# A two-block transformer on one core: Hyena spectra loaded earlier, the position network in halves, a head's memory softmax in one batch

## The chip, the core and the metric

The kernel runs on one core of a Trainium2 chip. A time is the device time of one execution in microseconds; runs of one kernel are compared by their median. TensorE (PE in the rows) does the matmuls; VectorE (DVE), ScalarE (ACT) and GpSimd (POOL) work on tiles beside it; SyncE (SP) issues all DMAs from one queue, in order. Each engine runs its own program in order and meets the others only at semaphores.

## The reference, cut to what matters

All is float32, 512 tokens by 1024 features. The first block: a hybrid mixer, a memory attention, a squared-ReLU MLP. The second: latent attention with a convolutional feed-forward network, then a Hyena mixer with another. The change touches five places:

```python
u = a * jax.nn.sigmoid(g)                      # short-convolution branch of the hybrid mixer
u = causal_depthwise_conv(u, conv_w, conv_b)   # 31 taps
log_f = jax.nn.log_sigmoid(f_logit + b_forget)
...
q = (h @ w_mq).reshape(B, S, MEM_HEADS, MEM_HEAD_DIM)       # memory attention: 4 heads, 256 slots
logits = jnp.einsum("bqhd,bmhd->bhqm", q, k) * (MEM_HEAD_DIM ** -0.5)
p = jax.nn.softmax(logits, axis=-1)
out = jnp.einsum("bhqm,bmhd->bqhd", p, v)
...
h = jnp.sin(freq * (z @ fw1 + fb1))            # Hyena position network, 64 wide, 512 positions
h = jnp.sin(freq * (h @ fw2 + fb2))
h = jnp.sin(freq * (h @ fw3 + fb3)) @ fw_out
...
u = dwconv_centred(x @ w_in, w_short)          # Hyena input and its width-3 convolution
v, g1, g2 = jnp.split(u, 3, axis=-1)
for o, gate in enumerate((g1, g2)):
    k_f = jnp.fft.rfft(two_sided_kernel(...), n=n)
    y = jnp.fft.irfft(jnp.fft.rfft(z, n=n) * k_f, n=n)[:, :length]
    z = gate * (y + d_bias[o] * z)
```

## The kernel before, in words

Features lie on the 128 partitions and tokens along the free axis, mostly in tiles of 128x512. Every product of float32 matrices is three matmuls of rounded halves (`mm3`, L127): each operand is split in a high part, which ACT copies, and a low part, which another engine gets by subtraction. All weights come in chunks of up to 1 MB (`CHUNKS`, numbered in the order of use) through two buffers: SP loads a chunk to `W32`, ACT makes `WH`, POOL makes `WL`; for chunks in `SHARED`, DVE makes the second half of `WL` (its `weights`). The load of chunk n waits until the low part of chunk n-2 is made, and ACT's copy waits until PE has used chunk n-2. Nothing is scheduled: the order on each engine is the order in which the functions `tensor_program`, `scalar_program`, `vector_program`, `pool_program` and `sync_program` write it, and a wait stops all that stands behind it on its engine.

The places, in order of time. **Position network** (0 to 21 us): three layers, each one matmul of 64x512 on PE (plain float32), three DVE instructions that reduce the angle (`layer`) and a sine on ACT (`sine`); the third sine is split to `H3H` and `H3L`, and `make_h` multiplies it with the output weights. POOL makes these weights (`wp`, `wp_low`) meanwhile. From it the filters and their spectra are computed (to 112 us), and the spectra are stored in memory as `kd`. **Forget gate** (112 to 152 us): PE makes the eight logits `f`, DVE scales them to `FZ`, PE turns them (`turn_f`), and DVE and ACT compute the log-sigmoid, whose cumulative sum is the matmul `cum`. This lies beside the first chunks of `win_ag` (numbers 2 to 5). In `gemm`, the argument `after` is called when a tile is complete, `between` after each step over k of the first chunk; `turn_f` is passed as `after`. **Memory attention** (451 to 512 us): `mem_q` makes the queries of a head, `mem_s` its logits in four blocks of 128x256, `mem_soft` and `mem_exp` the softmax, `mem_t` turns the probabilities, `mem_pv` multiplies with the values. There is one probability tile `PM`. DVE takes block after block: maximum, scale, wait for ACT's exponential, reciprocal, multiply; ACT can do the next block only after DVE has found its maximum. **Hyena** (1560 to 1860 us): twelve chunks `hy_in` with the width-3 convolution on DVE (`hyu`), then for each of two orders o: the transform of z (`dft_z`, 16 groups `zf` of six matmuls), the product with the spectrum on DVE (four instructions for each of eight pieces (m, c)) with sums to `YF` on POOL, and the inverse transform (`dft_i`). The product reads `KB[m % 2]` (1 MB each, in place of `X`, which is parked in memory as `xd` before) and, for m = 0, `KX`; both are loaded from `kd`. Piece (m = 2) waits for a load that may be issued when m = 0 is done. SP's program names chunks by number: it loads up to number 118, then `KX`, 119 and the four `KB` of order 0, then 120, `KX`, 121 and the four `KB` of order 1. The numbers stand for other chunks than the text around them suggests: `dft_z` and `dft_i` are 116 to 119 and `hy_o` is 120 to 123.

Of the kernel before, what the change touches and what calls it, by code (L numbers as in the profile page):

```python
# [63 lines left out]
CH = {}  # L64
# [5 lines left out]
SHARED = {n for n in range(1, len(CHUNKS)) if CHUNKS[n - 1][2] < 1000 or CHUNKS[n][:2] == ("hy_o", 1)}  # L70

# [175 lines left out]
def build(nc, t):  # L247
# [9 lines left out]
    with es:  # L257
# [82 lines left out]
        PM = sb("PM", A + 88, [128, 4, 256])  # L340
# [39 lines left out]
        KX = sb("KX", A + 112, [128, 1024])  # L380
# [43 lines left out]
        def tensor_program(pe):  # L424
# [180 lines left out]
            gemm("ag", CH["win_ag"][0:2], 8, 2, feat, lambda k: ("hn", 0, k), turn_f)  # L605
# [144 lines left out]
            def mem_s(h):  # L750
                for i in range(4):
                    ps = open_bank("ms_", h, i)
                    pe.wait_ge(*at("qm", h))
                    pe.wait_ge(*at("km", h))
                    pe.mm3(ps[:, 0:256], QMH[:, h, blk(i)], QML[:, h, blk(i)], KMH[:, h, :], KML[:, h, :],
                           True, True).then_inc(*up(acc, ("ms_", h, i)))

            def mem_t(h):
                for j in range(2):
                    ps = open_bank("mt", h, j)  # L760
                    for i in range(4):
                        pe.wait_ge(*at("mp", h, i))
                        ins = pe.turn(ps[:, blk(i)], PM[:, i, blk(j)], IDT[:])
# [258 lines left out]
        def scalar_program(act):  # L1022
# [1732 lines left out]
```

## Time and profile before

| | us |
|---|---|
| median of 3 runs (2318.22 to 2323.59) | 2319.98 |
| the profiled execution | 2320.62 |
| its span, first to last instruction | 2318.8 |
| PE busy | 2122.0 |
| DVE busy | 1324.6 |
| POOL busy | 946.0 |
| ACT busy | 836.1 |

Busy is the time in which an engine works on an instruction; a wait stands in square brackets behind the row of the instruction that waited, with the engine and tile that ended it. The mean granted TensorE clock is 0.939 of full speed (2.4 GHz).

### The profile page before, as it was taken

To read this page: it belongs to the slowest core of one execution; us is meant where nothing else is said; L and a number is where in the kernel's file an instruction comes from. 1 tells how busy PE (TensorE), PEld (TensorE's weight loads), DVE (VectorE), ACT (ScalarE), POOL (GpSimd) and SP (SyncE) were. 2 spreads that over 40 slices of the span, in tenths; PEclk is the share of its full clock that TensorE was granted. 3 is DMA by queue.
4 is the path that set the end of the run, shared out by engine and by line. 5 is a ranking of instruction groups with operands and counts; after the bars stand their busy time and mean duration, and the time that the engine had idled before them with its cause. 6 is when DMAs were issued, how large, how long until landed. Compare 5 with 4: busy or idle time off the path is not lost.

```text
span 2318.8 us, 23115 instructions
## 1 busy us (share of the span) xinstructions
PE 2122.0 (92%) x9475; PEld 1725.2 (74%) x9475; DVE 1324.6 (57%) x1631; ACT 836.1 (36%) x1175; POOL 946.0 (41%) x388
## 2 busy tenths in 40 slices
PE   7989988778999998899989999999987789999997
PEld 4667766667888886677778887877866677888786
DVE  6756762544324543456267776536656837777744
ACT  4623454444122223467243333223321224333322
POOL 4243124616444436211434434434655544334432
PEclk9989778888999998999999999989988898999998
DMA  5322111201222222111212222223231221322230
GB/s 179 142 85 75 46 37 55 91 26 66 104 96 91 93 107 71 39 32 53 73 55 91 91 100 100 91 73 122 95 138 68 105 73 55 101 99 91 94 106 37
DMA packets 34558, 194.02 MB, mean 84 GB/s; under 512 B 3903, under 2 KB 4495, under 8 KB 14932
## 3 DMA queue, kind: packets, MB, share of 16 engines
q1 hardware_dynamic: 34452, 192.54, 23.8%
q8 instruction: 75, 1.23, 0.2%
q14 instruction: 31, 0.25, 0.0%
HBM read 178.82 MB, written 13.64 MB: 83 GB/s over the span
## 4 chain that ended last, share of the span: by engine, by line
PE 59%; DVE 23%; ACT 11%; POOL 4%; issue 2%; DMA 1%; SPq 0%; DVEq 0%; POOLq 0%; ACTq 0%
PE ps L127 53%; DVE TMP L156 9%; DVE TMP L162 6%; PE ps L126 5%; ACT WH L143 4%; ACT TMP L144 1%; POOL WL L150 1%; DVE TMP L150 1%; DVE X L150 1%; ACT PAD L143 1%; POOL X L150 1%; DVE VG L150 1%; PE ps L135 1%; POOL YF L150 1%; DMA KB<-kd 1%
## 5 line engine op out<-in xcount | busy, mean ns | idle before, releaser
L150 POOL TENSOR_TENSOR WL<-W,WH 128x2048 fp32r<-128x2048 f32 (+3 forms) x175 | 710.1, 4062 | 1063.5 <-ACT WH L143 1063.5
L127 PE MATMUL ps<-HH,WL 128*128 128x512 f32 x1456 | 587.3, 403 | 64.3 <-ACT WH L143 18.2
L127 PE MATMUL ps<-HL,WH 128*128 128x512 f32 x1456 | 578.9, 398 | 0.0
L127 PE MATMUL ps<-HH,WH 128*128 128x512 f32 x1456 | 577.8, 397 | 0.0
L143 ACT ACTIVATE WH<-W 128x2048 fp32r<-128x2048 f32 (+2 forms) x157 | 291.8, 1859 | 322.0 <-PE ps L127 322.0
L127 PEld LDWEIGHTS ps<-HH,WL 128*128 128x128 f32 x1456 | 281.2, 193 | 137.3 <-issue 50.8
L127 PEld LDWEIGHTS ps<-HH,WH 128*128 128x128 f32 x1456 | 280.5, 193 | 60.8
L127 PEld LDWEIGHTS ps<-HL,WH 128*128 128x128 f32 x1456 | 281.3, 193 | 56.8 <-issue 0.2
L150 DVE TENSOR_TENSOR MRL<-MID,MRH 128x512 fp32r<-128x512 f32 x76 | 177.4, 2366 | 162.4 <-ACT MRH L143 162.4
L156 DVE TENSOR_SCALAR TMP<-PAD,PAR 128x512 f32<-128x512 f32 x88 | 208.9, 2374 | 70.6 <-ACT PAD L143 70.6
L127 PE MATMUL ps<-MRH,WL 128*128 128x512 f32 x608 | 238.4, 392 | 4.5 <-DVE TMP L162 2.2
L127 PE MATMUL ps<-MRH,WH 128*128 128x512 f32 x608 | 236.6, 389 | 0.0
L127 PE MATMUL ps<-MRL,WH 128*128 128x512 f32 x608 | 236.6, 389 | 0.0
L127 PEld LDWEIGHTS ps<-MRH,WL 128*128 128x128 f32 x608 | 114.1, 188 | 30.1 <-ACT PAD L143 3.0
L162 DVE SCALAR_TENSOR_TENSOR TMP<-PAD,PAR,TMP 128x512 f32<-128x512 f32 x176 | 132.3, 752 | 6.2
L127 PEld LDWEIGHTS ps<-MRH,WH 128*128 128x128 f32 x608 | 114.1, 188 | 24.1
L127 PEld LDWEIGHTS ps<-MRL,WH 128*128 128x128 f32 x608 | 114.1, 188 | 23.7 <-issue 0.5
L143 ACT ACTIVATE PAD<-ps 128x512 f32<-128x512 f32 x88 | 51.9, 590 | 193.4 <-PE ps L127 193.3
L150 POOL TENSOR_TENSOR TMP<-TMP,TMP 128x512 f32<-128x512 f32 x54 | 71.0, 1315 | 81.4 <-ACT TMP L144 79.3
L168 DVE RECIPROCAL SM<-SM 128x4 f32<-128x4 f32 (+2 forms) x46 | 7.9, 171 | 161.5 <-ACT SM L144 140.6
L162 DVE SCALAR_TENSOR_TENSOR X<-X,ps 128x512 f32<-128x512 f32 x32 | 22.0, 687 | 128.6 <-PE ps L127 128.4
L144 ACT ACTIVATE TMP<-TMP 128x512 f32<-128x512 f32 (+1 forms) x51 | 32.2, 632 | 157.5 <-DVE TMP L162 142.9
(337 smaller groups left out, 3159.4 us busy)
## 6 DMA issues: line engine op xcount, KB each, us to landing
W<-in_up SPq DMA_DIRECT2D x44, 1024.0 KB, 4.8
W<-in_down SPq DMA_DIRECT2D x22, 1024.0 KB, 4.8
W<-in_w_up SPq DMA_DIRECT2D x16, 1024.0 KB, 4.8
W<-in_w_down SPq DMA_DIRECT2D x16, 1024.0 KB, 4.8
W<-in_hy_in SPq DMA_DIRECT2D x12, 1024.0 KB, 4.9
kd<-STG SPq DMA_DIRECT2D x36, 256.0 KB, 2.0
KB<-kd SPq DMA_DIRECT2D x8, 1024.0 KB, 6.2
W<-in_win_ag SPq DMA_DIRECT2D x4, 1024.0 KB, 5.2
```

The costliest lines, as they stand in the source:

```text
L126: return self.eng.matmul(out, lhs, rhs, start=start, stop=stop, skip_group_check=True)
L127: return self.eng.matmul(out, lhs, rhs, start=start, stop=stop)
L135: return QUIET if self.eng is None else self.eng.transpose(out, src, ident)
L143: return self.eng.activation(out, src, fn, scale=scale)
L144: return self.eng.activation(out, src, fn, scale=scale, bias=bias)
L150: return QUIET if self.eng is None else self.eng.tensor_tensor(out, a, b, op)
L156: return self.eng.tensor_scalar(out, a, s1, None, o1)
L162: return self.eng.scalar_tensor_tensor(out=out, in0=a, scalar=s, in1=b, op0=o1, op1=o2)
L168: return QUIET if self.eng is None else self.eng.reciprocal(out, src)
```

## The change

Five edits.

1. SP loads the Hyena spectra earlier: the first `KB` and the `KX` of order 0 behind the sixth `hy_in` load, the second `KB` behind the seventh, `KX` and the first two `KB` of order 1 ahead of `dft_i` of order 1. Chunks are now named by `CH[...]`, not by number. `KX` has a tile of its own for each order, and `xd` is stored one chunk earlier.
2. The two `dft_i` chunks are in `SHARED`: POOL makes half of their `WL` and DVE the other half, ahead of its products.
3. The position network works on two halves of 256 columns, and the angle is kept in the matmul's bank.
4. `turn_f` is passed as `between`, and ACT copies chunk 3 ahead of the log-sigmoid.
5. Memory attention: two blocks of logits share a bank, one maximum instruction covers two blocks, the scale, the reciprocal and the exponentials of a head each go as a batch, the multiplication by the reciprocal is ACT's (`mem_norm`), `PM` is doubled, and the heads overlap more.

```diff
+SHARED |= set(CH["dft_i"])
...
-        PM = sb("PM", A + 88, [128, 4, 256])
+        PM = [sb(f"PM{i}", A + (72, 88)[i], [128, 4, 256]) for i in range(2)]
...
-        KX = sb("KX", A + 112, [128, 1024])
+        KX = [sb(f"KX{o}", (36, A + 112)[o], [128, 1024]) for o in range(2)]
...
             for l in range(3):
+                for c in range(2):
+                    p = slice(256 * c, 256 * c + 256)
...
+                        pe.wait_ge(*at("sin", l - 1, c))
...
+                    pe.mm(ps[0:64, 0:256], lhs, rhs, True, True).then_inc(*up(acc, ("mlp", l, c)))
...
-            gemm("ag", CH["win_ag"][0:2], 8, 2, feat, lambda k: ("hn", 0, k), turn_f)
+            gemm("ag", CH["win_ag"][0:2], 8, 2, feat, lambda k: ("hn", 0, k), between=turn_f)
...
             mem_s(0)
             mem_q(2)
+            mem_s(1)
+            mem_t(0)
+            mem_q(3)
             for h in range(4):
-                mem_t(h)
+                if h < 2:
+                    mem_s(h + 2)
+                mem_pv(h)
                 if h < 3:
-                    mem_s(h + 1)
-                if h == 0:
-                    mem_q(3)
-                mem_pv(h)
+                    mem_t(h + 1)
...
             sine(0)
+            sine(1)
             wp_high(0, 0, 0)
-            sine(1)
+            sine(2)
+            for c in range(2):
+                p = slice(256 * c, 256 * c + 256)
+                act.wait_ge(*at("sin", 2, c))
+                high(H3H[:, p], TMP[0][0:64, p], ("fh3", c))
             wp_high(0, 0, 1)
-            sine(2)
-            act.wait_ge(*at("sin", 2))
-            high(H3H[:], TMP[0][0:64, :], ("fh3",))
...
             scale_out(0)
+            weights(3)
...
-            weights(3)
             gate(0)
...
+            def mem_norm(h):
+                for i in range(4):
+                    s, p = 32 * (h % 2) + 168 + i, PM[h % 2][:, i, :]
+                    act.wait_ge(*at("rcp", "ms_", h))
+                    act.act(p, p, ACT.Identity, SM[:, s:s + 1]).then_inc(*out(("mp", h, i)))
...
+                for c in range(2):
+                    p = slice(256 * c, 256 * c + 256)
+                    arg, kq = bank("mlp", l, c)[0:64, 0:256], TMP[4][0:64, p]
...
+                s = 32 * (h % 2) + 160
+                for b in range(2):
+                    dve.wait_ge(*at("ms_", h, b))
+                    dve.rmax(SM[:, s + 2 * b:s + 2 * b + 2],
+                             bank("ms_", h, b)[:].rearrange("p (a c) -> p a c", a=2)).then_inc(*out())
+                dve.wait_ge(*now(dve_tile))
+                dve.tt(SM[:, s:s + 4], SM[:, s:s + 4], SM[:, 24:28], ALU.mult).then_inc(*out(("max", "ms_", h)))
+                dve.wait_ge(*at("exp", "ms_", h, 3))
+                dve.recip(SM[:, s + 8:s + 12], SM[:, s + 4:s + 8]).then_inc(*out(("rcp", "ms_", h)))
...
             for o in range(2):
+                weights(CH["dft_i"][o])
                 for m in range(4):
...
+            load_kb(0, 0)
+            load_kx(0)
+            weights(first + 6)
+            load_kb(0, 1)
+            weights(*range(first + 7, CH["dft_i"][0] + 1))
+            load_kb(0, 2)
+            load_kb(0, 3)
+            weights(CH["dft_z"][1])
+            load_kx(1)
+            load_kb(1, 0)
+            load_kb(1, 1)
+            weights(CH["dft_i"][1])
+            load_kb(1, 2)
+            load_kb(1, 3)
+            weights(*CH["hy_o"][0:2])
```

The order of instructions at three places. First ACT, from the end of the spectra to the first sigmoid; `WH_52` and `WH_53` are the high parts of chunks 2 and 3, the three `SM` rows of 128x32 the log-sigmoid. Before:

```order
L143 ACTIVATE WH_52<-W_0_50 128x2048
L144 ACTIVATE SM<-ps,PAR 128x4
L143 ACTIVATE TMP_67<-ps 128x512
L144 ACTIVATE SM<-SM 128x32
L144 ACT_TABLE_LOAD
L144 ACTIVATE SM<-SM 128x32
L144 ACT_TABLE_LOAD
L144 ACTIVATE SM<-SM,PAR 128x32
L143 ACTIVATE WH_53<-W_1_51 128x2048
L144 ACT_TABLE_LOAD
L144 ACTIVATE TMP_63<-TMP_63 128x512
```

And with the change:

```order
L144 ACTIVATE WH_52<-W_0_50 128x2048
L145 ACTIVATE SM<-ps,PAR 128x4
L144 ACTIVATE TMP_67<-ps 128x512
L144 ACTIVATE WH_53<-W_1_51 128x2048
L145 ACTIVATE SM<-SM 128x32
L145 ACT_TABLE_LOAD
L145 ACTIVATE SM<-SM 128x32
L145 ACT_TABLE_LOAD
L145 ACTIVATE SM<-SM,PAR 128x32
L145 ACT_TABLE_LOAD
L145 ACTIVATE TMP_63<-TMP_63 128x512
```

The copy of chunk 3 has moved past the three log-sigmoid instructions and their two table loads. On PE the transposes of `FZ`, on whose result the log-sigmoid waits, stood at the end of the 48 matmuls of chunk 2:

```order
L127 MATMUL ps<-HH,WH_52 128x512
L135 MATMUL ps<-IDT,FZ 128x8 x4
L127 MATMUL ps<-HH,WL_54 128x512
L127 MATMUL ps<-HL,WH_52 128x512
L127 MATMUL ps<-HH,WH_52 128x512
L135 MATMUL ps<-IDT,EB 128x16
L127 MATMUL ps<-HH,WL_55 128x512
```

With the change they stand behind its first six matmuls, and those of `EB` six further on:

```order
L128 MATMUL ps<-HH,WH_52 128x512
L136 MATMUL ps<-IDT,FZ 128x8 x4
L128 MATMUL ps<-HH,WL_54 128x512
L128 MATMUL ps<-HL,WH_52 128x512
L128 MATMUL ps<-HH,WH_52 128x512
L128 MATMUL ps<-HH,WL_54 128x512
L128 MATMUL ps<-HL,WH_52 128x512
L128 MATMUL ps<-HH,WH_52 128x512
L136 MATMUL ps<-IDT,EB 128x16
```

Last SP, around the Hyena spectra; `W_0_50` and `W_1_51` are the two `W32` buffers, `KB_185` and `KB_186` the two `KB`. Before, from the last `hy_in` load to the first two `KB` of order 1:

```order
L180 DMA W_1_51<-in_hy_in 128x2048
L180 DMA W_0_50<-in_dft_z 128x2048
L180 DMA W_1_51<-in_dft_i 128x2048
L180 DMA W_0_50<-in_dft_z 128x2048
L180 DMA KX<-kd 128x1024
L180 DMA W_1_51<-in_dft_i 128x2048
L180 DMA KB_185<-kd 128x2x1024
L180 DMA KB_186<-kd 128x2x1024
...
L180 DMA W_0_50<-in_hy_o 128x2048
L180 DMA KX<-kd 128x1024
L180 DMA W_1_51<-in_hy_o 128x2048
L180 DMA KB_185<-kd 128x2x1024
```

With the change, where `KB_187` and `KB_188` are the same two tiles, from the sixth `hy_in` load on:

```order
L181 DMA W_1_51<-in_hy_in 128x2048
L181 DMA KB_187<-kd 128x2x1024
L181 DMA KX_179<-kd 128x1024
L181 DMA W_0_50<-in_hy_in 128x2048
L181 DMA KB_188<-kd 128x2x1024
...
L181 DMA W_1_51<-in_dft_i 128x2048
L181 DMA KB_187<-kd 128x2x1024
L181 DMA KB_188<-kd 128x2x1024
L181 DMA W_0_50<-in_dft_z 128x2048
L181 DMA KX_180<-kd 128x1024
L181 DMA KB_187<-kd 128x2x1024
L181 DMA KB_188<-kd 128x2x1024
L181 DMA W_1_51<-in_dft_i 128x2048
```

The first two `KB` of order 0 stood behind the load of 119, whose buffer is free when POOL has split chunk 117; those of order 1 behind that of 121, whose buffer is free when POOL has split chunk 119. Now neither does.

## Rows read from the trace of the kernel before

**Rows 1.** The page, part 1: busy time, share of the span, instructions.

```profile
PE 2122.0 (92%) x9475; PEld 1725.2 (74%) x9475; DVE 1324.6 (57%) x1631; ACT 836.1 (36%) x1175; POOL 946.0 (41%) x388
```

**Rows 2.** A stretch: busy PE, PEld, DVE, ACT, POOL; granted clock, DMA share, GB/s.

```profile
470.00:515.00 45.00, 32.59 (x147) 26.01 (x146) 24.80 (x71) 21.75 (x46) 5.05 (x2) 0.85 0.07 24
```

**Rows 3.** Timeline of the start: start, us, engine, instruction, [idle before, releaser].

```profile
3.54 1.94 PE L127 MATMUL ps<-TMP,SM 33*64 33x512 f32 x2 [3.54 <-DMA TMP<-in_zfeat]
...
6.42 0.42 DVE L156 TENSOR_SCALAR TMP<-TMP 64x512 f32<-64x512 f32 x1
...
8.28 1.96 PE L127 MATMUL ps<-TMP,SM 64*64 64x512 f32 x2 [2.81 <-ACT TMP L144]
9.87 2.48 POOL L150 TENSOR_TENSOR STG<-FW 64x512 f32<-64x512 f32 x2 [9.43 <-DMA FW<-in_fw_out]
...
11.19 1.45 DVE L156 TENSOR_SCALAR TMP<-TMP 64x512 f32<-64x512 f32 x1
...
15.01 1.96 PE L127 MATMUL ps<-TMP,SM 64*64 64x512 f32 x2 [4.78 <-ACT TMP L144]
...
21.41 0.79 PE L127 MATMUL ps<-WPH,H3L 64*128 64x512 f32 x1 [4.43 <-DVE H3L L150]
```

**Rows 4.** Groups by form, ACT: busy us, mean ns of one.

```profile
L143 ACT ACTIVATE HM<-TMP 128x256 fp32r<-128x256 f32 x8 | 3.3, 417 | 7.3 <-DVE TMP L162 7.3
```

**Rows 5.** Groups by form, DVE.

```profile
L150 DVE TENSOR_TENSOR KML<-ps,KMH 128x256 fp32r<-128x256 f32 x4 | 1.5, 418 | 0.7 <-ACT KMH L143 0.7
```

**Rows 6.** Timeline of chunk 2's low part.

```profile
111.85 1.22 DVE L150 TENSOR_TENSOR WL<-W,WH 128x1024 fp32r<-128x1024 f32 x1 [3.48 <-ACT WH L143]
111.89 3.38 POOL L150 TENSOR_TENSOR WL<-W,WH 128x1024 fp32r<-128x1024 f32 x1 [2.37 <-ACT WH L143]
```

**Rows 7.** Timeline of the forget gate, chunks 2 and 3.

```profile
127.31 0.41 PE L135 MATMUL ps<-IDT,FZ 8*128 8x8 f32 x4
...
131.49 1.89 ACT L143 ACTIVATE WH<-W 128x2048 fp32r<-128x2048 f32 x1
...
138.06 0.76 PE L127 MATMUL ps<-HH,WL 128*128 128x512 f32 x1 [9.29 <-ACT WH L143]
...
138.62 0.63 PE L127 MATMUL ps<-HL,WH 128*128 128x512 f32 x1
...
142.73 0.40 PE L127 MATMUL ps<-HH,WH 128*128 128x512 f32 x1
```

**Rows 8.** Groups by form, memory attention (466 to 513 us): exponential, its sum, maximum.

```profile
L141 ACT ACTIVATE PM<-ps,SM 128x256 f32<-128x256 f32 x16 | 9.0, 565 | 19.4 <-DVE SM L157 19.4
...
L141 ACT ACTIVATION_READ_ACCUMULATOR PM<-ps,SM 128x1 f32 x16 | 3.1, 191 | 0.0
...
L171 DVE TENSOR_REDUCE SM<-ps 128x1 f32<-128x256 f32 x16 | 6.7, 416 | 0.0
```

**Rows 9.** Timeline of memory attention, last two heads.

```profile
493.70 0.33 PE L135 MATMUL ps<-IDT,PM 128*128 128x128 f32 x1 [1.52 <-DVE PM L156]
...
510.34 0.63 PE L127 MATMUL ps<-OMH,WL 128*128 128x512 f32 x1
```

**Rows 10.** Timeline of Hyena, order 0.

```profile
1705.77 4.80 POOL L150 TENSOR_TENSOR WL<-W,WH 128x2048 fp32r<-128x2048 f32 x1 [6.08 <-ACT WH L143]
...
1711.28 0.90 SPq L180 DMA_DIRECT2D KB<-kd  x2
...
1718.39 1.88 DVE L150 TENSOR_TENSOR TMP<-ps,KB 128x512 f32<-128x512 f32 x3 [12.27 <-DMA KB<-kd]
1719.76 2.51 POOL L150 TENSOR_TENSOR YF<-TMP,TMP 128x512 f32<-128x512 f32 x2 [9.19 <-DVE TMP L150]
```

**Rows 11.** Timeline of Hyena, order 1.

```profile
1785.14 4.60 POOL L150 TENSOR_TENSOR WL<-W,WH 128x2048 fp32r<-128x2048 f32 x1 [3.75 <-ACT WH L143]
...
1797.77 1.89 DVE L150 TENSOR_TENSOR TMP<-ps,KB 128x512 f32<-128x512 f32 x3 [13.78 <-DMA KB<-kd]
```

**Rows 12.** Tile KB: time from issue to landing.

```profile
DMA to landing us min/median/max: 4.8/6.2/9.3
```

More of the change, by code:

```diff
@@ L1331, in mem_exp, with mem_turned @@
             def mem_exp(h):
+                slot = 32 * (h % 2) + 160
                 for i in range(4):
-                    need = [("mt", h - 1, 1)] if h else []
-                    expo(("ms_", h, i), PM[:, i, :], 256, SM[:, 20 + i:21 + i], 32 * (h % 2) + 160, *need)
-            mq_high(0)
-            mq_high(1)
-            root(("st", 1), 0, "eps6")
-            mem_exp(0)
-            mq_high(2)
-            for h in range(4):
+                    if h >= 2:
+                        act.wait_ge(*at("mt", h - 2, 1))
+                    act.wait_ge(*at("max", "ms_", h))
+                    act.act(PM[h % 2][:, i, :], bank("ms_", h, i // 2)[:, 256 * (i % 2):256 * (i % 2) + 256], ACT.Exp,
+                            SM[:, 20 + i:21 + i], SM[:, slot + i:slot + i + 1], SM[:, slot + 4 + i:slot + 5 + i]).then_inc(
+                        *out(("exp", "ms_", h, i), *[("free", "ms_", h, i // 2)] * (i % 2)))
+            def mem_norm(h):
[3 more added lines that the diff above has]
+                    act.act(p, p, ACT.Identity, SM[:, s:s + 1]).then_inc(*out(("mp", h, i)))
+            def mem_turned(h):
                 for j in range(2):
@@ L1346, in scalar_program, with mem_out @@
                     high(PMH[:, j, :], bank("mt", h, j)[:], ("pm", h, j))
-                if h < 3:
-                    mem_exp(h + 1)
-                if h == 0:
-                    mq_high(3)
+            def mem_out(h):
                 act.wait_ge(*at("mo", h))
                 high(OMH[:, h, :], bank("mo", h)[:], ("om", h))
+            mq_high(0)
+            mq_high(1)
+            root(("st", 1), 0, "eps6")
+            mem_exp(0)
+            mem_norm(0)
+            mq_high(2)
+            mem_exp(1)
+            mem_turned(0)
+            mem_norm(1)
+            mq_high(3)
+            for h in range(4):
+                if h < 2:
+                    mem_exp(h + 2)
+                mem_out(h)
+                if h < 3:
+                    mem_turned(h + 1)
+                if h < 2:
+                    mem_norm(h + 2)
             roots_next()
@@ L1719, in vector_program @@
                 layer(l)
-            low(H3L[:], TMP[0][0:64, :], H3H[:], ("fh3",))
+            for c in range(2):
+                p = slice(256 * c, 256 * c + 256)
+                low(H3L[:, p], TMP[0][0:64, p], H3H[:, p], ("fh3", c))
             for n in range(17):
@@ L2542, in sync_program, with load_kx, load_kb @@
             load("pos", POSI[:], t["pos"])
-            weights(*range(60, 108))
+            def load_kx(o):
+                for k in (8, 9, 26, 27)[2 * o:2 * o + 2]:
+                    sp.wait_ge(*at("kd", k))
+                for i in (22, 23):
+                    if o:
+                        sp.wait_ge(*at("hyu", i))
+                sp.dma(KX[o][:], KD[o, 8]).then_inc(*up(kx_land, ("kx", o), by=16))
+            def load_kb(o, m):
+                if m >= 2:
+                    sp.wait_ge(*at("kbu", o, m - 2))
+                elif o:
+                    sp.wait_ge(*at("kbu", 0, m + 2))
+                else:
+                    sp.wait_ge(*at("xs"))
+                for k in range(36):
+                    sp.wait_ge(*at("kd", k))
+                sp.dma(KB[m % 2][:].rearrange("p (a c) -> p a c", a=2),
+                       KD[o, 2 * m:2 * m + 2].rearrange("a p c -> p a c")).then_inc(
+                    *up(kb_land[m % 2], ("kb", o, m), by=16))
+            first = CH["hy_in"][0]
+            weights(*range(60, first + 3))
             for k in range(8):
@@ L2572, in sync_program @@
             load("xl", X[:], XD)
[L2573 removed]
+            weights(*range(CH["hy_o"][2], len(CHUNKS)))
             for k in range(8):
```

111 lines of the change are left out of this document (45 added, 66 removed).

## The prediction

> **What bounds the kernel now.** First the page's busy times: PE works for 2122.0 of 2318.8 us and no other engine for more than 1325 [rows 1]. No matmul of size is removed, so only the 197 us in which PE stands idle can be won, and an edit on DVE, ACT or POOL counts where PE waits for it. Then the timelines of the five places, read for the idle time in front of PE's instructions. At the start PE's three layers begin at 3.54, 8.28 and 15.01 and the first filter matmul at 21.41; each waits for ACT's sine or DVE's `H3L` [rows 3]. In the forget gate PE stops for 9.29 us at 138.06, for `WH` of chunk 3, which ACT began only at 131.49 [rows 7]. In memory attention PE works 32.59 of 45 us [rows 2] and waits 1.52 us for one block of `PM` after the other [rows 9]. In Hyena's two orders DVE stands 12.27 and 13.78 us for `KB` alone [rows 10, 11], and POOL's sums and the inverse transform behind it.
>
> **Hyena (gain 21.2).** In order 0 the low part of chunk 117 runs 1705.77 to 1710.57, the first `KB` is issued at 1711.28, and the products start at 1718.39 [rows 10]. With the load some 60 us ahead, DVE has all it needs when it falls idle, at 1718.39 − 12.27 = 1706.12. The change gives it half of `WL` first: 1.22 for 1024 columns [rows 6], so it is ready at about 1707.4. POOL, which makes the first sum 1.37 us behind the first product (1719.76), takes 3.38 for its half in place of 4.80 [rows 6, 10] and is free at 1705.77 + 3.38 = 1709.15. So the first sum comes at 1709.15 and not 1719.76: 10.6. In order 1 the low part starts at 1785.14, is done at 1788.5, and the first sum stood at 1797.77 + 1.37 = 1799.14 [rows 11]: again 10.6. Without the split (4.80 and 4.60) each would be 9.2 to 9.4. What is late next is `KB` for m = 2: it may be issued when m = 0 is done and is needed after m = 1, and a piece (m, c) takes DVE some 2.7 us, its three products of 1.88 [rows 10] and the one with `KX`; that cover is some 6.6 us with the queue's delay, for a landing of 4.8 to 9.3 [rows 12]. It was so before too, so I take no change; if transfers now collide, up to 9.3 − 6.6 = 2.7 each time. The four loads moved ahead, and the store of `X`, lie among loads of `hy_in`, where POOL waits 6.08 us for work [rows 10]: a `KB` of 9.3 us at the worst could push one chunk by 3.2 us, which stands under rivals. Sum 21.2, with bounds 17 (one late landing of 2.7 and 1.5 lost elsewhere) and 22.
>
> **Forget gate (gain 11.3).** `turn_f` after six matmuls instead of 48: DVE's `FZ` is ready by about 116, PE gets there near 118, and each transpose group is 0.41 [rows 7], as before. ACT's copy of chunk 3 no longer stands behind a chain that begins with those transposes at 127.31; it follows the scaling at 115.4, runs 1.89, and is done near 117.3. POOL's full `WL` of 4.80 (that of another chunk of the same size [rows 10]) then ends near 122, and PE is through with chunk 2 at 138.06 − 9.29 = 128.77. So the whole 9.29 goes. After the stall PE ran ten matmuls slow: they last 0.63 where the later ones last 0.40, and start 0.43 apart in place of 0.23, from 138.06 to the one at 142.73 [rows 7]: 2.0. Sum 11.3. Next late: chunk 4's copy waits until PE has used chunk 2, at 128.8, not for the log-sigmoid; two chunks take it and POOL 1.89 + 4.80 = 6.7, to 135.5, and PE needs it at about 141. The log-sigmoid itself now runs beside chunk 3, with 20 us until `cum`. At the least 9 (POOL's copy slips and the slow stretch stays), at the most 12.
>
> **Position network (gain 6.1).** A layer now has two halves. To the first half's sine: PE about 1.1 (half of the 1.94 for 512 columns, and a start) [rows 3]; three DVE instructions of 256 columns, priced by one that reads 256 columns of a bank, 0.42 [rows 5], with gaps 1.46; a sine of 256 columns at 0.42 [rows 4], with its wait 0.5. Together 3.1, and DVE is occupied 2.92 for both halves, just inside it. Three layers from 3.54: 12.9; the second half follows 1.5 later, at 14.4; the splits `H3H` and `H3L` of a half take 0.42 each, so both halves are ready at 15.3, against 21.41 [rows 3]. Before, a layer took 8.28 − 3.54 = 4.74 alone, and 6.73 once POOL worked beside it: the same DVE instruction went from 0.42 at 6.42 to 1.45 at 11.19, with POOL's 2.48 from 9.87 [rows 3]. I take that this slowing doesn't come back, since the half instructions read at most one operand outside the bank; if it does, 2 us of the gain go (4). The spectra, ACT's first copies and the rest start as much earlier, and no load of the first 16 us is waited for. Bounds 4 and 7.
>
> That the slowing goes agrees with the Trainium skill, "SBUF — State Buffer", section on the two separate sides: VectorE and GpSimd take their common port pair as an exclusive lock, held by a VectorE operation in a two-port mode or with two SBUF inputs, and one with a single SBUF input outside those modes doesn't contend. The rows show the slow pair; that a bank operand frees it, none shows. Against the change speaks its page "VectorE: DVE Perf Modes", section on why PSUM operands drop a tier: a PSUM operand takes the fast mode from a float32 instruction. The trace agrees: 0.42 buys 512 columns in SBUF [rows 3] but 256 from a bank [rows 5]. An estimate by that rule is some 0.15 us lost on each layer's second instruction; it is within the 0.42 above.
>
> **Memory attention (gain 6.0).** Before, a head costs four times a chain of maximum 0.416, scale, exponential 0.565 and its sum 0.191, reciprocal, multiply [rows 8]; PE sees it as 0.33 + 1.52 = 1.85 per block [rows 9], 7.4 a head. Now a head is two maxima over 512 columns (0.7 each, taken as less than two of 0.416), one scale 0.2, four exponentials with sums at about 0.62 = 2.5, one reciprocal 0.2, four multiplications on ACT at 0.42 [rows 4] = 1.6: 5.9 in a row. Each waits on shared ACT and DVE with three more copies per head (`mem_turned`, `mem_out`). Placed by the written order from 466.5 on, with matmuls unchanged: head 0 is turned at 474.0, head 1 at 483, head 2 at 491.4, head 3 at 497.7; `PML` of head 3 is ready at 502.3, and the first output matmul starts at 504.1, against 510.34 [rows 9]. Heads 2 and 3 leave PE idle some 4 and 2 us before their turns, so part of it runs at the lower clock, as before (mean 0.85 [rows 2]). Bounds 3 (an exponential costs its full 0.76, and multiplications 0.5: 0.9 a head on three heads) and 8 (clock stays up).
>
> **The sum.** 21.2 + 11.3 + 6.1 + 6.0 = 44.6. The profiled execution took 2320.62; 2320.62 − 44.6 = 2276.0. Its time is 0.64 above the median of the runs, so I say 2275.5. These stretches are apart in time and the rest of the program is written as before, so they add. Low bounds 17 + 9 + 4 + 3 = 33, high 22 + 12 + 7 + 8 = 49: 2271 to 2287 if all go one way, so 2272 to 2281 for this case.
>
> **Rivals.**
> - *The wait comes back in Hyena.* `KB` for m = 2 (or the order-1 load at its new place beside a weight load) lands after its need. For it: landings reach 9.3 us [rows 12]. Against it: the same loads stood there before. 2.7 us at each of two places, or one order's 10.6 lost to half: 2281 to 2286.
> - *Attention gives nothing.* The longer waits in one piece let the granted clock fall more often, and every copy on ACT queues behind a batch. For it: clock 0.85 already [rows 2], and ACT gets the multiplications. Against it: 7.4 against 5.9 a head. With start contention left: 2275.5 + 6 + 2 = 2283.5, range 2280 to 2286.
> - *More than counted.* Fewer stops keep PE at full speed beyond the ten matmuls, and the first half of the last layer lets PE begin before 15.3. 5 to 8 us more: 2268 to 2271.
> - *The change doesn't do what it says.* The loads are earlier but the products wait for something else that landed at the same time (`KX`, the store of `X`, a bank). Against it: both rows name `KB` [rows 10, 11]. 2297.
> - *Slower.* SP's queue is in order: `KB` and `KX` wait for the store of `X` and for the stored spectra, with the `hy_in` loads queued behind them, and ACT, POOL and PE wait for those. Two `KB` at 9.3 and one `KX` of half the size, with no slack, is 23 us on the path, and if the products of both orders still wait as before, the 21.2 isn't had: 2320 − 23.4 + 23 = 2320, and with 4 us of slower clock behind those stops 2324. It decides once a chunk comes 6.08 us late, where POOL's idle time ends [rows 10], and needs this at nearly every load.
>
> **How the numbers follow.** Main case 0.69, wait back in Hyena 0.11, attention 0.09, more 0.06, not what it says 0.02, the slower case 0.03. The time is the main case's, 2275.5. The range reaches from the favourable rival's 2268 to past the two nearest on the other side: 2266 to 2288 holds all but some 0.15. A measurement tells 0.2% (4.6 us) from no change: the slower case lies at 2320 to 2324, a third of it within that bound, so slower 0.02, same 0.01, faster 0.97.
>
> **What would show it.** Right: first filter matmul near 15.3; DVE's angle instructions near 0.42 also beside POOL; no `WH` wait of 9 us near 130; first output matmul of memory attention some 23.5 us earlier than 510.34 (near 487 with the two gains before it); no `<-DMA KB` ahead of a product with m = 0, and the first `YF` 3.4 us behind the start of POOL's half. Wrong: idle time of several microseconds on PE inside `hy_in`, new `<-DMA W` or `<-DMA KB` waits, or PE busy well above 2122 from a lower clock.

## The result and the profile after

| | us |
|---|---|
| before, median of 4 runs (2318.22 to 2323.59) | 2320.34 |
| changed, median of 4 runs (2281.91 to 2287.43) | 2285.58 |
| ratio, with its 95% interval | 0.9847 (0.983 to 0.9864) |
| the profiled execution of the changed kernel | 2287.43 |
| the same kernel run five times more later (2280.11 to 2286.90) | 2286.13 |

The forecast was 2275.5 with 2266 to 2288. Over all nine runs the changed kernel's median is 2286.13; that is the base for the experiments below. Against 2320 some 34 to 35 us are gained, where 44.6 were forecast. Part 1 of the page after, which answers to [rows 1]:

```profile
PE 2118.8 (93%) x9481; PEld 1725.2 (75%) x9481; DVE 1327.9 (58%) x1596; ACT 842.3 (37%) x1195; POOL 942.6 (41%) x388
```

PE's busy time is 3.2 us shorter; the other 30.0 of the 33.2 us by which the span is shorter (2318.8 to 2285.6) come out of its idle time. To see where, both executions are cut at the same matmuls: at numbers 0, 100, 200, 300, 400, 500, 1100 and 1200 of the matmuls of `HH` with `WL` (not shown: 300 to 400 took 68.0 in both, 500 to 600 and 600 to 1100 gave 1.1 and 1.3). The columns are the stretch, its length, busy time of PE, PEld, DVE, ACT and POOL, the granted clock of TensorE, the DMA share and GB/s. Before:

```profile
0.00:115.40 115.40, 96.39 (x359) 65.63 (x359) 82.13 (x123) 61.50 (x108) 40.50 (x31) 1.00 0.46 162
115.40:244.50 129.10, 117.55 (x472) 91.75 (x473) 76.19 (x125) 41.19 (x60) 43.60 (x14) 0.88 0.21 77
244.50:554.80 310.30, 255.32 (x1098) 205.99 (x1097) 158.12 (x286) 146.75 (x270) 124.38 (x62) 0.81 0.16 55
554.80:624.60 69.80, 69.80 (x317) 58.06 (x316) 30.45 (x37) 14.43 (x12) 29.02 (x7) 1.00 0.22 76
692.60:1107.40 414.80, 386.73 (x1787) 316.95 (x1786) 198.46 (x246) 184.50 (x288) 141.72 (x46) 0.98 0.20 68
...
1700.40:1993.00 292.60, 242.43 (x1200) 203.50 (x1198) 189.64 (x261) 80.36 (x97) 144.01 (x90) 0.90 0.25 90
1993.00:2318.80 325.80, 309.55 (x1395) 253.88 (x1394) 212.44 (x177) 102.20 (x117) 127.34 (x32) 0.98 0.26 88
```

And after:

```profile
0.00:111.50 111.50, 99.27 (x364) 67.92 (x364) 82.59 (x133) 62.23 (x113) 39.82 (x31) 1.00 0.48 167
111.50:229.80 118.30, 114.05 (x472) 89.40 (x473) 78.69 (x126) 41.52 (x60) 43.80 (x14) 0.93 0.23 83
229.80:530.70 300.90, 250.88 (x1098) 203.00 (x1097) 148.12 (x239) 151.11 (x285) 123.92 (x61) 0.82 0.16 56
530.70:604.20 73.50, 71.68 (x317) 59.17 (x316) 35.37 (x37) 14.76 (x12) 29.41 (x8) 0.98 0.22 74
672.20:1092.50 420.30, 393.01 (x1788) 321.70 (x1787) 199.07 (x246) 184.86 (x288) 141.72 (x46) 0.96 0.20 67
...
1683.10:1957.40 274.30, 236.67 (x1199) 200.62 (x1199) 194.34 (x263) 80.37 (x97) 140.95 (x90) 0.93 0.24 87
1957.40:2285.60 328.20, 311.86 (x1395) 256.29 (x1394) 212.57 (x177) 102.20 (x117) 127.40 (x32) 0.97 0.25 87
```

The four stretches that hold edits give 3.9 + 10.8 + 9.4 + 18.3 = 42.4. Three stretches in which nothing was edited take back 3.7 + 5.5 + 2.4 = 11.6, each with a lower clock than before. That second sum is what the forecast didn't have.

**Start.** PE's first filter matmul (21.41 before [rows 3]) and DVE's angle beside POOL, which works from 9.41:

```profile
9.88 0.42 DVE L157 TENSOR_SCALAR TMP<-ps 64x256 f32<-64x256 f32 x1
10.33 0.41 DVE L163 SCALAR_TENSOR_TENSOR TMP<-TMP,ps 64x256 f32<-64x256 f32 x1
...
15.17 0.79 PE L128 MATMUL ps<-WPH,H3L 64*128 64x512 f32 x1 [2.81 <-DVE H3L L151]
```

6.2 us earlier, and the DVE instructions aren't slowed. By 111.5 only 3.9 is left: behind the next stall (27.32; 33.54 before) fifteen matmuls took 0.63 us each, where five did before. The clock column shows 1.00 there all the same, so they are known as slow by their durations alone.

**Forget gate.** ACT's copy of chunk 3 begins at 111.48 and the transposes of `FZ` at 113.11, neither behind the other; the wait of 9.29 [rows 7] is gone. DVE's instruction at 115.39 took 0.17 before the change, with POOL idle; now it lies beside POOL's split of 113.47 to 118.06. And a new wait has come, at the matmul of the cumulative sum:

```profile
111.48 1.90 ACT L144 ACTIVATE WH<-W 128x2048 fp32r<-128x2048 f32 x1
...
113.11 0.41 PE L136 MATMUL ps<-IDT,FZ 8*128 8x8 f32 x4
...
115.39 2.70 DVE L157 TENSOR_SCALAR SM<-SM 128x32 f32<-128x32 f32 x1
...
136.47 2.31 PE L128 MATMUL ps<-TMP,SM 128*8 128x512 f32 x8 [1.94 <-DMA TMP<-in_consts]
```

**Memory attention.** The first output matmul stands at 488.27, against 510.34 [rows 9]: 22.1 earlier, of which 14.5 were there at the first logits (465.46 before, 450.97 after). So 7.6 is attention's own. One instruction sticks out, DVE's scale of head 1's maxima, of four columns:

```profile
459.75 4.60 POOL L151 TENSOR_TENSOR WL<-W,WH 128x2048 fp32r<-128x2048 f32 x1 [18.35 <-ACT WH L144]
...
462.10 2.26 DVE L151 TENSOR_TENSOR SM<-SM 128x4 f32<-128x4 f32 x1
...
488.27 0.40 PE L128 MATMUL ps<-OMH,WL 128*128 128x512 f32 x1
```

It ends at 464.36, POOL's at 459.75 + 4.60 = 464.35; in the other heads it takes 0.16. That one of the two engines waits like this until the other's instruction is over is what the expectations below call the port.

**Behind attention.** In the stretch of 73.5 us (69.8 before) stands the same thing on the path. DVE adds up eight squares, in seven sums; before, the last of them had begun when POOL began to split a chunk:

```profile
559.76 2.94 DVE L150 TENSOR_TENSOR Y<-Y 128x512 f32<-128x512 f32 x4
...
562.46 4.67 POOL L150 TENSOR_TENSOR WL<-W,WH 128x2048 fp32r<-128x2048 f32 x1 [6.33 <-ACT WH L143]
```

After, POOL began 0.01 us ahead of the last sum:

```profile
538.39 4.57 POOL L151 TENSOR_TENSOR WL<-W,WH 128x2048 fp32r<-128x2048 f32 x1 [5.87 <-ACT WH L144]
...
538.40 5.10 DVE L151 TENSOR_TENSOR Y<-Y 128x512 f32<-128x512 f32 x1
...
543.56 1.05 PE L127 MATMUL ps<-ONE,Y 128*128 128x1 f32 x8 [1.82 <-DVE Y L151]
```

**Hyena.** No product waits for `KB` any more. Order 0, which answers to [rows 10], and order 1, which answers to [rows 11]:

```profile
1688.54 2.59 POOL L151 TENSOR_TENSOR WL<-W,WH 128x1024 fp32r<-128x1024 f32 x1 [6.07 <-ACT WH L144]
1688.80 3.42 DVE L151 TENSOR_TENSOR WL<-W,WH 128x1024 fp32r<-128x1024 f32 x1
...
1692.14 1.87 DVE L151 TENSOR_TENSOR TMP<-ps,KB 128x512 f32<-128x512 f32 x3
...
1693.49 5.26 POOL L151 TENSOR_TENSOR YF<-TMP,TMP 128x512 f32<-128x512 f32 x4 [2.36 <-DVE TMP L151]
...
1758.12 1.23 DVE L151 TENSOR_TENSOR WL<-W,WH 128x1024 fp32r<-128x1024 f32 x1 [1.11 <-ACT WH L144]
1758.16 3.43 POOL L151 TENSOR_TENSOR WL<-W,WH 128x1024 fp32r<-128x1024 f32 x1 [3.75 <-ACT WH L144]
...
1761.78 1.29 DVE L151 TENSOR_TENSOR TMP<-ps,KB 128x512 f32<-128x512 f32 x2 [1.83 <-PE ps L128]
...
1762.55 5.26 POOL L151 TENSOR_TENSOR YF<-TMP,TMP 128x512 f32<-128x512 f32 x4 [0.95 <-DVE TMP L151]
```

From the start of the low part to the first sum it was 1719.76 − 1705.77 = 13.99, and in order 1 13.99 again (1797.77 + 1.36 − 1785.14). Now it is 4.95 and 4.39: 9.0 and 9.6 gained, where the forecast had 10.6 twice. The two halves aren't made side by side: whichever engine starts second takes longer by what the first still has to do (POOL's 2.59 and then DVE's 3.42; DVE's 1.23 and then POOL's 3.43). In order 1 PE's transform is late next, 1.83 us. `KB` lands no later than it did (4.8/6.2/9.3 before [rows 12]):

```profile
DMA to landing us min/median/max: 4.8/5.1/7.6
```

### The profile page after: what moved, and what is told of

It is laid out like the page before. It is cut to its first block, busy times and chain, and to the rows that moved or that the text cites. A ratio compares the mean times of both kernels' runs of the same rounds, so it can differ in the third digit from the quotient of the medians.

```text
span 2285.6 us, 23112 instructions
## 1 busy us (share of the span) xinstructions
PE 2118.8 (93%) x9481; PEld 1725.2 (75%) x9481; DVE 1327.9 (58%) x1596; ACT 842.3 (37%) x1195; POOL 942.6 (41%) x388
## 3 DMA queue, kind: packets, MB, share of 16 engines
q8 instruction: 75, 1.23, 0.2%
## 4 chain that ended last, share of the span: by engine, by line
PE 59%; DVE 23%; ACT 11%; POOL 4%; issue 2%; DMA 0%; SPq 0%; DVEq 0%; POOLq 0%; ACTq 0%
PE ps L128 54%; DVE TMP L157 9%; DVE TMP L163 6%; PE ps L127 5%; ACT WH L144 4%; DVE TMP L151 1%; ACT TMP L145 1%; POOL X L151 1%; POOL WL L151 1%; ACT PAD L144 1%; PE ps L136 1%; DVE X L151 1%; DVE VG L151 1%; POOL YF L151 1%; POOL TMP L151 1%
## 5 line engine op out<-in xcount | busy, mean ns | idle before, releaser
L169 DVE RECIPROCAL SM<-SM 128x4 f32<-128x4 f32 (+1 forms) x34 | 6.0, 176 | 155.2 <-ACT SM L145 136.4
L151 DVE TENSOR_TENSOR TMP<-ps,TMP 128x512 f32<-128x512 f32 x36 | 24.9, 690 | 113.8 <-PE ps L128 105.5
```

The lines of the kernel that those rows point to most:

```text
L151: return QUIET if self.eng is None else self.eng.tensor_tensor(out, a, b, op)
L169: return QUIET if self.eng is None else self.eng.reciprocal(out, src)
```

## The experiments

All twelve start from the changed kernel and are compared with its median of nine runs, 2286.1. Two theories went into the first four, which each put one part back. Theory 1: a part is worth what PE's start times show at its place. Theory 2: part of each gain is paid back later. Medians of four or five runs are compared with a base that itself spreads over 7.3 us, so a difference of a few microseconds is judged by the place in the profile and not by the time.

**1. Hyena put back.** The edit takes back the SP order, the second `KX` and the split of `dft_i`:

```diff
-SHARED |= set(CH["dft_i"])
-                weights(CH["dft_i"][o])
-            load_kb(0, 0)
-            load_kx(0)
 ...
+                weights(119 + 2 * o)
+                for m in range(4):
```

> The changed kernel with the Hyena part put back: SP loads the spectra in the old order, one KX, POOL makes the whole low part of the two dft_i chunks. Theory 1 (each part is worth what PE's local start times show in the profiled execution of the changed kernel): 19.6 us slower than the changed kernel, 2305 us, with a wait of DVE for KB of 12 to 14 us back in both orders. Theory 2 (part of each gain is paid back elsewhere by PE's lower clock in unchanged code): the loss is 12 to 16, 2298 to 2301. My prediction's own term would make it 21.2 slower, 2307.

Measured: 2303.0 (2297.65 to 2306.05), 16.9 slower; ratio to before 0.9923 (0.991 to 0.9936). The idle time of DVE ahead of products, us and times:

```profile
  DMA KB<-kd: 25.7, 2
```

The wait is KB's, as forecast, and the part is worth some 17, below the 18.3 of its stretch by no more than runs differ. That lies between the two theories (2305, and 2298 to 2301) and decides for neither. This is the largest term and nearly all of it arrives.

**2. Forget gate put back.**

```diff
-            gemm("ag", ..., between=turn_f)
+            gemm("ag", ..., turn_f)
             scale_out(0)
-            weights(3)
 ...
+            weights(3)
             gate(0)
```

> The changed kernel with turn_f again at the end of chunk 2 and ACT's copy of chunk 3 behind the log-sigmoid. Theory 1: 9.3 us of wait and 2 us of slow matmuls come back, the wait of 1.9 us for the triangle goes: 9.5 to 10 slower than the changed kernel, 2295. Theory 2: 5 to 8 slower, 2291 to 2293. The prediction's term: 11.3, 2297.

Measured: 2291.32 (2289.20 to 2293.47), 5.2 slower; ratio 0.9877 (0.9864 to 0.9891). The wait is back in full:

```profile
132.68 0.76 PE L128 MATMUL ps<-HH,WL 128*128 128x512 f32 x1 [9.30 <-ACT WH L144]
```

PE is 10.0 us later at 240 us (239.8 against 229.8) and still 10.3 at 682; the unedited stretch behind it takes 416.1 in place of 420.3, and at the end 3.9 are left in the profiled execution (2289.5 against 2285.6) and 5.2 in the medians. Theory 2 holds: half of what the place shows is gone by the end.

**3. Position network put back.**

```diff
-                for c in range(2):
-                    p = slice(256 * c, 256 * c + 256)
-                    ps = open_bank("mlp", l, c)
+                ps = open_bank("mlp", l)
```

> The changed kernel with the position network on all 512 columns, angle in TMP. Theory 1: the first filter matmul starts 6.2 us later, near 21.4, and the whole is 6 us slower, 2291.5. Theory 2: 12 matmuls that ran at the lower clock from 30.1 to 35.3 in the changed kernel run fast again, as before the change, which gives 2.4 back: 3.8 slower or less, 2288 to 2289.5.

Measured: 2287.39 (2286.97 to 2288.54), 1.3 slower; ratio 0.9862 (0.9847 to 0.9877). The first filter matmul and the unedited stretch that took 420.3 us in the changed kernel:

```profile
20.73 0.79 PE L128 MATMUL ps<-WPH,H3L 64*128 64x512 f32 x1 [4.44 <-DVE H3L L151]
```

```profile
677.50:1091.30 413.80, 385.70 (x1787) 315.91 (x1786) 198.45 (x246) 184.62 (x288) 141.72 (x46) 0.98 0.19 68
```

5.6 us later at the start, still 5.3 at 677, and 1.2 ahead of the changed kernel at 1091: the same code took 6.5 us less. My reason for theory 2 was wrong, though. The matmuls at 30 us didn't run fast again (fourteen slow, against fifteen); the difference came back a thousand microseconds later.

**4. Memory attention put back.**

```diff
-        PM = [sb(f"PM{i}", A + (72, 88)[i], [128, 4, 256]) for i in range(2)]
+        PM = sb("PM", A + 88, [128, 4, 256])
 ...
             for h in range(4):
-                if h < 2:
-                    mem_s(h + 2)
+                mem_t(h)
+                if h < 3:
+                    mem_s(h + 1)
+                if h == 0:
+                    mem_q(3)
                 mem_pv(h)
-                if h < 3:
-                    mem_t(h + 1)
 ...
```

> The changed kernel with memory attention as it was. Theory 1: the first output matmul comes 7.5 us later relative to the stage's start, and the whole is 7.5 slower, 2293. Theory 2: the new DVE wait behind attention (1.8 us at 543.6, where POOL works beside DVE's squares) and the slow matmuls near 545, 935 and 960 are consequences of attention's new timing, and go: 0 to 4 slower, 2286 to 2289. The prediction's term: 6.0, 2291.5.

Measured: 2288.89 (2287.22 to 2293.59), 2.8 slower; ratio 0.987 (0.9857 to 0.9883). The stage is 9.9 longer, but the one behind it takes 69.9 again, without the wait of 1.82. Theory 2 again: with the new attention the last sum of squares meets POOL's split. The profiled execution was the slowest of the four (2293.59), so the size of this part is known to a few microseconds only. The four parts cost 16.9 + 5.2 + 1.3 + 2.8 = 26.2 one at a time, and all together 34.

**5. The changed kernel again**, without an edit.

> The changed kernel itself, word for word, to say how far executions of one program differ and to give the four undone parts a firmer base. If the four losses (17.4, 5.7, 1.8 and 3.3, sum 28.2) fall short of the whole gain of 34.8 by an unlucky base, this median lies 1 to 3 us below 2285.6; if they fall short because the parts' gains don't add, it lies at 2285.6 within 1.

Measured: 2286.13 (2280.11 to 2286.90). The base wasn't unlucky, by the expectation's own test. That the parts don't add is less firm than the medians make it look: the nine runs seem to lie in two groups, two at 2280 to 2282 and seven at 2285 to 2287.5, and with means in place of medians the four parts cost 30 against 35 for all together, a difference that these few runs don't tell from none. What the traces do show are the places where a gain is lost again.

**6. The triangle first.**

```diff
-            weights(4, 5, 6)
+            weights(4, 5)
             sp.wait_ge(*at("rs", 0))
             load("tri", DG[:], t["consts"][:, 256:768])
+            weights(6)
```

> The changed kernel with the load of the triangle (the tile of the cumulative sum) moved ahead of the load of chunk 6. Theory: the wait of PE for it, 1.94 us at 136.5, is an effect of the forget gate's gain, since the load stands in SP's queue behind a load that waits for the split of chunk 4; it goes, and the whole is 1.9 us faster, about 2283.7. Rival: something else of the cumulative sum is late right behind it, and under 0.5 us is gained.

Measured: 2278.80 (2277.51 to 2279.19), 7.3 faster; ratio to before 0.9822 (0.9806 to 0.9837). The wait is gone, but 100 matmuls further on only 0.5 us of it is left (229.3 against 229.8), since more of them ran slow. The two unedited stretches, which took 73.5 and 420.3 in the changed kernel, gave 9.2, of which little was lost again behind them (the spans are 2277.0 and 2285.6):

```profile
530.60:600.40 69.80, 69.80 (x317) 58.08 (x316) 30.80 (x37) 14.76 (x12) 29.72 (x7) 1.00 0.23 77
668.40:1083.20 414.80, 386.74 (x1788) 316.84 (x1787) 198.48 (x246) 184.48 (x288) 141.72 (x46) 0.98 0.19 68
```

Here DVE's last sum began before POOL's split, and POOL waited for it (5.03 in place of 4.57). Neither theory in the expectation foresaw this: the edit moved what follows by a little (530.6 against 530.7 at the start of that stage), and the order of two engines turned.

**7. The scale of the maxima as four instructions.**

```diff
-                dve.tt(SM[:, s:s + 4], SM[:, s:s + 4], SM[:, 24:28], ALU.mult)...
+                for i in range(4):
+                    ins = dve.ts(SM[:, s + i:s + i + 1], SM[:, s + i:s + i + 1], SM[:, 24 + i:25 + i], None, ALU.mult)
```

> The changed kernel with the scaling of a head's maxima, one DVE instruction with two operands in SBUF (128x4), as four instructions with one each (128x1). Theory (the port): the 2.26 us that this instruction took at 462.1 while POOL split a chunk were a wait for POOL, and the four take 0.9 together there; attention gains about 1.4 there and loses 0.5 on each of the other heads, 0 to 1 us in sum. Rival (the instruction was slow for another reason, such as its operands being just written): the four take more than 2 us there as well.

Measured: 2284.03 (2283.21 to 2288.44), 2.1 less than the base, which four runs don't tell from no change; ratio 0.9849 (0.9832 to 0.9866). Head 1, in the midst of POOL's split:

```profile
465.21 0.58 DVE L157 TENSOR_SCALAR SM<-SM 128x1 f32<-128x1 f32 x4
```

0.58 for four in place of 2.26 for one: the theory holds and the rival falls. It doesn't follow that one operand in SBUF never waits. In the changed kernel a TENSOR_SCALAR of 128x32 from SBUF to SBUF took 2.70 beside POOL's split and 0.17 without (the row of 115.39), and run 10 shows another. From the first logits to the first output matmul it is 37.6 us, against 37.3: what head 1 gains, the other three heads' 0.4 each take back.

**8. POOL behind the last sum.**

```diff
             post(2, Y2)
+            pool.wait_ge(*at("hacc", 2, 7))
             weights(CH["w_down"][-1] + 1)
```

> The changed kernel with one wait more: behind memory attention POOL splits chunk 26 only when DVE has added the last of the eight squares, 0.7 us later. Theory (the port): the last add took 5.10 us at 538.4 because it began 0.01 us behind POOL's split of 4.57 us; it takes 0.68 again, PE's wait of 1.82 us at 543.6 and the slow matmuls behind it go, and the stage takes 69.9 us as before the change instead of 73.5: 3.6 faster, about 2282. Rival: the stage is longer for another reason (clock), and the kernel is the same or 0.7 slower.

Measured: 2282.57 (2280.15 to 2284.70), 3.6 faster; ratio 0.9839 (0.9821 to 0.9856). DVE's seven sums, POOL's split, and the stage:

```profile
534.07 5.11 DVE L151 TENSOR_TENSOR Y<-Y 128x512 f32<-128x512 f32 x7
...
539.27 4.60 POOL L151 TENSOR_TENSOR WL<-W,WH 128x2048 fp32r<-128x2048 f32 x1 [6.65 <-DVE Y L151]
```

```profile
530.70:600.60 69.90, 69.90 (x318) 58.09 (x316) 31.03 (x37) 14.75 (x12) 29.52 (x8) 1.00 0.22 77
```

A wait added to an engine with time to spare gives 3.6 us back to PE: shown at the place. The time agrees, but all four runs, two near 2280.3 and two near 2284.7, lie inside the base's own spread, and run 9 shows a larger difference from an edit worth 0.1; the time alone proves little. The unedited stretch behind 668 us took 419.8, nearly as in the changed kernel.

**9. `dft_i` not shared.**

```diff
-SHARED |= set(CH["dft_i"])
-                weights(CH["dft_i"][o])
```

> The changed kernel without the split of the two dft_i chunks: POOL makes the whole low part. Theory (the port): where POOL and DVE make a half each, they don't work at once, 2.59 and then 3.42 less the wait in order 0, so halves end 3.7 us after the start and not 3.38 or 1.22; POOL alone needs 4.6. The first sum of order 0 comes 0 to 0.3 us later, that of order 1 0.2 to 0.5 later, and the kernel is within 1 us of the changed one, 2285 to 2287. The prediction had the split worth 1.2 to 1.4 in each order: 2288.5.

Measured: 2280.81 (2279.43 to 2288.67), ratio 0.9835 (0.9812 to 0.9858). From the start of the low part to the first sum, in order 0:

```profile
1683.89 4.82 POOL L150 TENSOR_TENSOR WL<-W,WH 128x2048 fp32r<-128x2048 f32 x1 [6.07 <-ACT WH L143]
...
1688.67 2.53 POOL L150 TENSOR_TENSOR YF<-TMP,TMP 128x512 f32<-128x512 f32 x2
```

4.78, against 4.95 with the split; in order 1 4.66 against 4.39. By its places edit 2 is worth 0.1 us. The time lies 5 below the base, where 2285 to 2287 was expected, but 4.2 of it is again in the unedited stretch behind 672 us (416.1 us), so it is no verdict on the edit. Three of the four runs lie at 2279.4 to 2281.4 and one at 2288.7.

**10. The angle in SBUF.**

```diff
-                    arg, kq = bank("mlp", l, c)[0:64, 0:256], TMP[4][0:64, p]
+                    ps, kq = bank("mlp", l, c)[0:64, 0:256], TMP[4][0:64, p]
+                    arg = TMP[3 if l == 1 else 0][0:64, p]
 ...
```

> The changed kernel with the angle of the position network kept in TMP, halves of 256 columns as they are. Theory (the port): the second and third DVE instruction are faster until 9.4 us (the second near 0.25 in place of 0.42), and slow once POOL begins at 9.4, one of them taking over 1 us; the first filter matmul starts at 16 to 17.5 in place of 15.17. Rival (halves alone give the whole gain, and the bank is no help or a loss): it starts at 14.5 to 15.2.

Measured in one run: 2285.29. POOL works from 9.40 here:

```profile
9.54 1.26 DVE L157 TENSOR_SCALAR TMP<-TMP 64x256 f32<-64x256 f32 x1
10.84 1.36 DVE L163 SCALAR_TENSOR_TENSOR TMP<-TMP,TMP 64x256 f32<-64x256 f32 x1
...
17.47 0.79 PE L128 MATMUL ps<-WPH,H3L 64*128 64x512 f32 x1 [3.66 <-DVE H3L L151]
```

Without POOL the same two take 0.28 and 0.42; beside it 1.26 and 1.36, and the first filter matmul is 2.3 us later than with the angle in the bank. So of the 6.2 us at the start, the halves give 3.9 and the bank 2.3.

**11. The low parts of `dft_i` on DVE.**

```diff
+POOL_PART = {n: 16 for n in CH["dft_i"]}
-                h = cols // 2
+                h = POOL_PART.get(n, cols // 2)
```

> The changed kernel with the low parts of the two dft_i chunks made by DVE but for 16 columns. Theory (the port): DVE alone takes 2.3 to 2.4 us for 2032 columns, less than the 3.5 that DVE and POOL need for it together; the first sum of order 0 comes 0.9 us earlier, that of order 1 is unchanged, since PE's transform is late there (DVE waits for it until 1761.8): 0.5 to 1 us faster, 2285. Rival (the two engines do work side by side): it is 1 us slower in each order, 2288.

Measured: 2282.27 (2279.97 to 2284.07), ratio 0.9833 (0.9818 to 0.9847). Order 0:

```profile
1687.17 0.42 POOL L152 TENSOR_TENSOR WL<-W,WH 128x16 fp32r<-128x16 f32 x1 [6.07 <-ACT WH L145]
1687.43 2.29 DVE L152 TENSOR_TENSOR WL<-W,WH 128x2032 fp32r<-128x2032 f32 x1
...
1691.00 5.25 POOL L152 TENSOR_TENSOR YF<-TMP,TMP 128x512 f32<-128x512 f32 x4 [3.41 <-DVE TMP L152]
```

3.83 from the start to the first sum in place of 4.95, and 4.71 for 4.39 in order 1: 0.8 gained in sum, as expected, though order 1 was expected to stay. There POOL's 16 columns began behind DVE's 2032 and took 2.31. DVE alone takes 2.29 for what the two together took 3.7 for. The rest of the 3.9 by which the median is lower comes from elsewhere: the stage behind attention took 69.9, and other unedited stretches differ by 2 to 4 us both ways.

**12. All four mended.** The edits of runs 6, 8 and 11, and that of run 7 for head 1 alone.

> The changed kernel with four edits: the triangle loaded ahead of chunk 6, POOL's wait behind the last sum of squares, the scale of head 1 alone as four instructions, and the low parts of dft_i on DVE. Theory: no wait of 1.9 at 136 and none of 1.8 at 543; against the changed kernel (2286) it gains 1.9 + 3.6 + 0.9 + 0.5 = 6.9, 2279; if the stretch behind 690 us comes out with 13 slow matmuls as in the run with the triangle first, and not 33, up to 5 more, 2274. Rival: the run with the triangle first (2278.8) already had all that is to be had, and this one is at 2278 to 2279.

Measured: 2277.12 (2275.05 to 2279.52), 9.0 below the changed kernel; ratio to before 0.9811 (0.9797 to 0.9826). Against the run with the triangle first it is 1.7 less, which isn't told apart: that kernel had the good outcome at both far places already, and here the unedited stretch took 417.3. The median lies between the 2279 and the 2274 of the theory, and below those of both kernels.

## Why the prediction was right, and where its sum was off

The direction, the main mechanisms and all five places held, and the time is in the range, 10 us above the value. That it is in the range is in part luck. The prediction gave its main case 2272 to 2281, and 2285.6 is outside; it lies where two rivals stood, `KB` late again in Hyena (2281 to 2286) and attention without a gain (2280 to 2286), and neither of them happened. By its steps:

- **Position network, 6.1.** The place gave 6.2, and the first filter matmul stood at 15.17 (15.3 forecast). That POOL's slowing goes with the angle in the bank was taken without a row; run 10 shows it: 2.3 us (2 forecast). The Trainium skill, "SBUF — State Buffer", section on the two separate sides, says the same of two SBUF inputs and of the two-port modes, and the trace agrees: 1.26 and 1.36 beside POOL for 0.28 and 0.42 without it. Its other rule, in "VectorE: DVE Perf Modes", section on why PSUM operands drop a tier, holds too: the second instruction takes 0.28 from SBUF and 0.42 from the bank, 0.14 where 0.15 was estimated, a small price for being free of POOL. The rows that the prediction compared for this rule were of two kinds of instruction, a TENSOR_SCALAR [rows 3] and a TENSOR_TENSOR [rows 5]; the like pair is in run 10. Of the 6.2 us, 3.9 are left at 111.5.
- **Forget gate, 11.3.** 9.3 and the slow stretch went, as said. I looked for what is late next at chunk 4, and missed the triangle, whose load SP holds behind that of chunk 6: 1.9 of it came back as a wait. 10.8 by its stretch.
- **Memory attention, 6.0.** 7.6 at the place; the prediction's own placing gives 510.34 − 504.1 = 6.2. The step that failed stands behind it: "these stretches are apart in time and the rest of the program is written as before, so they add". The new timing put a sum of squares 0.01 us behind POOL's split, which costs 3.6 to 3.7 (runs 4 and 8). The stage took 73.5 to 73.6 in the profiles of the changed kernel and of runs 1, 2, 3, 5 and 9, and 69.8 to 69.9 in all others.
- **Hyena, 21.2.** 18.3 to 18.6. The failed price is the two halves of a low part, 1.22 on DVE and 3.38 on POOL, taken as done side by side. [Rows 6] showed these two numbers, and POOL's 3.38 already held DVE's 1.22: half of 4.6 is 2.3. With 2.3 for POOL alone I would have seen that the halves are made one after the other, and that the split is worth 0.1 and not 2.6. POOL's lock, and a transform that is late by 1.8 in order 1, are the difference.
- **The unedited stretches.** Besides attention's 3.7, the stretch from matmul 400 to 500 took 5.5 more and the last one 2.4 more, at a lower clock in both. In the profiled executions of the changed kernel and the twelve runs the first of them took 413.8 to 420.3 us with the same instructions; 14 to 34 of its matmuls took 0.60 to 0.66 us, where 0.40 is the usual time. PE's waits agree up to 271 us into this stretch; from there the next 22 us are, before and after:

```profile
964.30:986.30 22.00, 17.34 (x80) 12.86 (x79) 15.56 (x27) 12.85 (x22) 5.08 (x2) 1.00 0.17 51
943.90:965.90 22.00, 17.93 (x55) 12.46 (x54) 12.87 (x20) 9.98 (x15) 5.04 (x2) 0.69 0.16 51
```

After the change the granted clock fell from 2.4 to 1.2 GHz in parts of these 22 us (0.69 in the mean), and PE got through 55 matmuls in place of 80. The rival with a lower clock (0.09) was of this kind, but I put it into attention, where the clock didn't fall. Of the changed kernel's nine executions two were profiled, both at 420; that this stretch makes the two groups of its times is likely and not shown. What decides which outcome an execution gets stays open. That it depends on small shifts in what comes before is likely, since the edit of run 6, at 119 us, is followed by the shorter outcome and by times that lie within 1.7 us of each other, where the changed kernel's spread over 7.3; it takes more executions to show it.
- No chunk of `hy_in` was held up by the spectra's loads, and the slower rival found nothing: the stretch up to matmul 1100 in which these loads are issued (1594.5 to 1700.4 before the change, 1577.2 to 1683.1 after) took 105.9 in both.

## What to carry to other kernels

Local gains of a few microseconds, read from an engine's start times, aren't what the whole kernel gains: the places showed 42 us here and 34 arrived, while a wait of 1.9 us taken away in run 6 was followed by 7.3. Price a change by its places, then look in the unedited code behind it for a near miss, two engines that pass each other by less than the shift, and give the one with time to spare a wait. A duration taken from a row in which two engines work at once may hold the other's time already: divide it by its size and compare with a row where the engine is alone.

## What the runs showed of the hardware

DVE and GpSimd shut each other out for whole instructions when both sides need the port, even an instruction of four columns (0.16 alone, 2.26 beside a split of 4.60) and one of 16 columns on GpSimd (0.42 with a start ahead of DVE's, 2.31 behind it, run 11). So the engines don't meet at semaphores only, as the description of the chip above has it. Not held were DVE instructions of one column with one tensor operand (0.58 for four) and those with an operand in a bank (0.42 beside POOL as without it). One SBUF operand alone isn't enough: a TENSOR_SCALAR from SBUF to SBUF was held with 256 columns (1.26 for 0.28, run 10) and with 32 (2.70 for 0.17). The second surprise is the clock: the same code came out 6.5 us apart (413.8 and 420.3) in executions that differed only in what was done some hundred microseconds before.
